# Two mixture-of-experts loops on one core: the first block written apart, and the pause moved from behind block 7 to behind block 12

## What is computed

```python
# first block: 16 experts, 2 of one group of 4 for each token, no biases
for e in range(N_EXPERTS):
    h = jax.nn.silu(t @ w_gate[e]) * (t @ w_up[e])
    y = y + gate_dense[:, e:e + 1] * (h @ w_down[e])

# second block: 32 experts, 4 for each token, with biases on both products
gu = xb @ w_gu[e] + b_gu[e]
gate, up = gu[:, :1024], gu[:, 1024:]
gate = jnp.minimum(gate, 7.0)
up = jnp.clip(up, -7.0, 7.0)
ys = ((up + 1.0) * gate * jax.nn.sigmoid(1.702 * gate)) @ w_down[e] + b_down[e]
```

## Time and profile before

| | us |
|---|---|
| median of three executions | 2166.97 |
| the profiled execution | 2168.93 |
| span of its trace | 2167.1 |
| TensorE matmul busy | 2088.0 (96%) |
| TensorE weight loads busy | 903.1 (42%) |
| VectorE busy | 517.2 (24%) |
| ScalarE busy | 318.1 (15%) |

### The profile page before, as it was taken

How to read it: one execution, slowest core, us unless ns; L and a number is a source line. 1 busy time by engine, 2 the same in 40 slices (tenths; PEclk the granted TensorE clock), 3 DMA queues, 4 the chain that set the end, 5 groups by cost and what they waited for, 6 DMA issues and landing times.

```text
span 2167.1 us, 22836 instructions
## 1 busy us (share of the span) xinstructions
PE 2088.0 (96%) x8939; PEld 903.1 (42%) x8942; DVE 517.2 (24%) x1098; ACT 318.1 (15%) x487; POOL 44.0 (2%) x67
## 2 busy tenths in 40 slices
PE   8999999999999999999999999999999999999997
PEld 6754333343324465645565433333333333333332
DVE  0675211011113410001052422222222122212212
ACT  1531111010002032211042111111110011111000
POOL 2010000000001000000000000000000000000000
PEclk9999999999999999999999999999999999999999
DMA  9984999999998422334334499999999999999997
GB/s 372 353 328 160 368 429 429 427 406 429 428 429 322 141 81 90 106 102 155 124 153 165 161 411 429 429 429 429 428 429 428 429 429 429 429 428 429 428 429 300
DMA packets 83290, 720.54 MB, mean 332 GB/s; under 512 B 6411, under 2 KB 11776, under 8 KB 42640
## 3 DMA queue, kind: packets, MB, share of 16 engines
q1 hardware_dynamic: 80864, 713.76, 79.7%
q0 software_dynamic: 2384, 6.21, 1.0%
HBM read 718.87 MB, written 1.08 MB: 332 GB/s over the span
## 4 chain that ended last, share of the span: by engine, by line
PE 62%; DMA 33%; DVE 3%; ACT 1%; issue 1%; POOL 0%; SPq 0%; DVEq 0%; ACTq 0%
DMA ring<-in_exp_w_gu 26%; PE bank L832 14%; PE bank L842 10%; PE bank L440 10%; DMA ring<-in_w_up 7%; PE bank L470 4%; PE bank L532 3%; PE bank L1078 3%; PE bank L457 3%; PE bank L1089 3%; PE bank L849 2%; PE bank L812 2%; PE bank L824 1%; PE bank L1214 1%; PE bank L793 1%
## 5 line engine op out<-in xcount | busy, mean ns | idle before, releaser
L832 PE MATMUL bank<-ring,pool 128*64 128x512 f32 x2560 | 566.0, 595 | 13.3 <-DMA ring<-in_w_up 10.3
L842 PE MATMUL bank<-ring,pool 128*64 128x512 f32 x2048 | 451.6, 595 | 23.1 <-DMA ring<-in_exp_w_gu 23.1
L832 PEld LDWEIGHTS bank<-ring,pool 128*64 128x64 f32 x2560 | 177.0, 137 | 356.2 <-issue 333.1
L842 PEld LDWEIGHTS bank<-ring,pool 128*64 128x64 f32 x2048 | 141.7, 137 | 309.9 <-issue 253.6
L440 PE MATMUL bank<-ring,pool 128*128 128x512 f32 (+2 forms) x512 | 213.3, 576 | 1.3 <-issue 1.3
L440 PEld LDWEIGHTS bank<-ring,pool 128*128 128x128 f32 x512 | 96.9, 190 | 112.9 <-issue 105.9
L1614 ACT ACTIVATE pool<-pool 128x512 f32<-128x512 f32 x32 | 20.1, 629 | 740.3 <-DVE pool L2284 740.3
L2284 DVE TENSOR_SCALAR pool<-bank 128x512 f32<-128x512 f32 x32 | 22.1, 691 | 417.0 <-PE bank L842 417.0
L1457 ACT ACTIVATE pool<-bank 128x512 f32<-128x512 f32 (+1 forms) x104 | 60.4, 580 | 325.9 <-PE bank L1141 63.9
L849 PE MATMUL bank<-pool,junk 64*128 64x512 f32 x400 | 99.4, 615 | 2.6 <-ACT pool L1457 1.1
L812 PE MATMUL bank<-pool 128*64 128x512 f32 x384 | 93.0, 605 | 0.1
(11 more groups left out here) (394 smaller groups left out, 1511.9 us busy)
## 6 DMA issues: line engine op xcount, KB each, us to landing
ring<-in_exp_w_gu SPq DMA_DIRECT2D x128, 2048.0 KB, 23.8
ring<-in_exp_w_down SPq DMA_DIRECT2D x64, 2048.0 KB, 20.0
ring<-in_w_gate SPq DMA_DIRECT2D x32, 2048.0 KB, 18.8
ring<-in_w_up SPq DMA_DIRECT2D x32, 2048.0 KB, 21.2
ring<-in_w_down SPq DMA_DIRECT2D x32, 2048.0 KB, 17.1
ring<-in_w_in SPq DMA_DIRECT2D x21, 2048.0 KB, 7.8
ring<-in_ada_w SPq DMA_DIRECT2D x12, 2048.0 KB, 16.8
ring<-in_w_out SPq DMA_DIRECT2D x4, 2048.0 KB, 10.5
```

Source lines behind the costliest of these rows:

```text
L832: i = mm(dst[half[f], :], chunks[kk], weights[j][:, k, f * 512:(f + 1) * 512], start=(kk == 0), stop=(kk == KC - 1))
L842: i = mm(dst[half[f], :], chunks[2 * j + k], weights[j][:, k, at:at + 512], start=False, stop=(j == 3 and k == 1))
```

## The change

`SPLIT` goes from 7 to 12. Body 0 of both loops is written out apart as `first_block`, in another order, and the loops start at 1:

- In both stages the gather of block 1 comes first, ahead of the waits for `y_slot` and `put`.
- In m1 there is no scatter; an empty instruction increments the semaphore that it would have.
- In m2 `biases` moves from between `turn_hidden` and `turn_gathered` to behind the down product.

```diff
-        SPLIT = 7
+        SPLIT = 12
...
+                def first_block():
+
+                    pe.wait_ge(S(f"{m}_pick"), 2)
+                    gather()
+                    pe.wait_ge(S(f"{m}_y_slot"), 1)
+                    pe.wait_ge(S(f"{m}_put"), 1)
+                    if biased:
+                        scatter()
+                    else:
+                        pe.nop().then_inc(S("m1_scattered"), 1)
+                    pe.wait_ge(S(f"{m}_hid"), 2)
+                    turn_hidden()
+                    pe.wait_ge(S(f"{m}_rows"), 2)
+                    turn_gathered()
+                    pe.wait_ge(S(f"{m}_hidT"), 1)
+                    for j in (4, 5):
+                        pe.wait_ge(full[j], 16)
+                        product(DN, hid_chunks, j)
+                    if biased:
+                        pe.wait_ge(S("m2_expert"), 2)
+                        biases()
+                    pe.wait_ge(S(f"{m}_pick_g"), 1)
+                    pe.wait_ge(S(f"{m}_xgT"), 2)
+                    turn_put()
+                    for j in range(4):
+                        pe.wait_ge(full[j], 32)
+                        up(j)
+
...
+                first_block()
                 if m == "m1":
-                    blocks(0, SPLIT)
+                    blocks(1, SPLIT)
...
                 else:
-                    blocks(0, n - 1)
+                    blocks(1, n - 1)
```

## The result

The changed kernel takes 2170.73 us, the kernel before 2168.28 us (medians of 20 executions each); 2.45 us apart; the ratio, as it was estimated with its interval, is 1.0015, 95% interval 1.0009 to 1.0021. That is 2.0 to 4.5 us slower (3.25 in the middle), a loss clear of noise but hardly beyond the 0.2% that I had called the edge of "no change". The forecast was 3.6 us more, 2170.6 us. That the time itself was met within 0.2 us is partly luck: the forecast stood on 2166.97 us, the median of three executions, and twenty give 1.3 us more.

What follows compares the result with a forecast made beforehand. The prediction took the stream of weight loads to bind some bodies of m1 and most of m2, TensorE the rest. +6.0 - 1.5 - 0.9 = +3.6 us on 2166.97 gave 2170.6 us, range 2168.0 to 2173.2.

Steps and rivals of the forecast that it cites:

- The pause (+6.0): m1: moved behind block 12, only three bodies follow to use up the stream's lead; 6.0 us more.
- Rival C: m1: the ring pays for the pause wherever it stands, leaving only the gains, -2.4 us, 2164.6 us; chance 0.08.
- the whole hole of 2.98 us: m1, behind the pause after block 7: the stream's loss there, taken as all that the pause costs before the change.
- The first block of m1 (-1.5): m1's body 0: removing the scatter closes the stream's hole at 244 to 250; 1.50 us gained, bounds 1.0 and 1.91.
- One premise: m1's body 0: from a load's issue to its first byte take about 1.5 us.
- The first block of m2 (-0.9): m2's body 0: fifth unit asked for 1.57 us earlier, less a new 0.7 us hole; 0.9 us gained.
- only 1.1 to 1.2 us are in hand: m2, second body's fifth unit: the margin before the stream runs dry, so the earlier start opens a 0.7 us hole.
- rival B: Second body's fifth unit: holes move instead of closing, loads starting earlier drain earlier; +4.8 or +6.3 us; chance 0.23.
- Rival D: Loops of m1 and m2: shifted code forces instruction fetches at jumps back, +11 to +61 us on top; chance 0.03.

Runs made afterwards that it cites:

- e2: Kernel before with SPLIT = 12; m2's body 0 apart with scatter and biases behind the down product; 1.004 times before's time, m1 451.28 us, m2 916.64.
- e1: Changed kernel with the pause back behind block 7 and m2's body 0 back in its loop; 1.0001 times before's time, m1 444.70 us, m2 913.81.
- e9: Changed kernel with the pause behind block 10 and half the products of m2's block 0 unit 3 left out; m1 445.12 us, m2 912.84.
- e3: Changed kernel with m1's body 0 scatter kept, pause behind block 10, m2's biases behind the down product in every body; 298.54 us to the pause, m2 914.61.
- e5: Changed kernel with pause behind block 8, gather ahead of scatter in all bodies, m2's biases last in all; 0.9986 times before's time, 2166.09 us.
- e6: Changed kernel with pause behind block 5 and half the products of m2's block 1 units 1 and 2 left out; m1 444.55 us, m2 914.83.

## Why the prediction was right, and where it was wrong

**The pause (+6.0): right in kind, up to a microsecond too large.** Behind it the changed kernel took 95.74 us where 15.09 + 3 x 26.90 = 95.8 stood in the sum, and the five bodies ahead of it were bound by the stream at 29.37 us, as 568.30 - 538.93 = 29.37 in the chain. The table of m1 shows the mechanism whole. From block 5 to block 9 the place doesn't matter, 444.35 to 444.72 us. From block 10 on it costs 0.5, 3.5 and 5.3 us over the mean of those four (444.58); by the prediction's way of adding up, 15.1 us and the bodies at 26.90 and 29.37 us, the three would cost 1.1, 3.5 and 6.0. The kernels that differ in m1 by the pause's place alone say 4.95 (e2 against before) and 5.16 us (changed against e1) for block 12. The rest of the 6.0 lies ahead of block 7's place, where executions of the same code differ by about 1 us (209.70 and 208.70 in before and e2). Block 2 is too early: the stream had not yet got a lead, and the hole was 9.0 us. Rival C, the ring absorbing the pause wherever it stands, is refuted by blocks 2, 11 and 12. One step of the prediction doesn't come out: it has the pause behind block 7 cost the whole hole of 2.98 us, but 236.63 us are only 1.7 more than eight bodies at the stream's 29.37; no run shows where the other 1.3 went.

**The first block of m1 (-1.5): right, its size within the noise.** To block 7's place the three kernels with the scatter took 208.70 to 210.43, mean 209.61; the seven others with a pause behind block 5 or later and the scatter gone took 207.27 to 208.40, mean 207.83. The difference is 1.8 us, and the kernels of one group differ by up to 1.7 and 1.1 us among themselves, so it can't be told from 1.91, all that the scatter took of TensorE, nor from 1.50. Pairs with the pause at one place say 1.6 (e1 against before), 1.4 (changed against e2) and 2.9 us (e9 against e3). In the two profiles that I compared first it is 2.4, which is partly chance. One premise was rough: by the trace's time stamps the first packet of block 1's first load starts 0.97 us behind its request, not 1.5; the 1.5 us also hold the slow start. e3 shows that it is the removal: with the scatter kept, the gather's place gave nothing. What I had not seen is that the loss in GB/s is a sum over 16 engines. Unit 3 of block 5 of m1 had landed on its last engine 142.5 to 144.4 us behind the first request with the scatter, 141.2 to 142.3 without, by the same time stamps as above.

**The first block of m2 (-0.9): wrong.** It gave +0.24 in the profile, and in no kernel with the same requests was it a gain. The step that failed is "only 1.1 to 1.2 us are in hand": that the hole at the first place shrinks by the 1.57 us of the earlier request, that the second body's fifth unit gives 0.7 us back, and that there is no third place. The row of the kernel before at 1284 shows that nothing was in hand at the second place: the stream dips to 396 GB/s there already. In the changed kernel it dips to 374, and to 396 at a third place (1265), where the kernel before moves 437. The reports say what became of the gain. At unit 4 of block 1 the mean of the 16 engines was 1.2 us earlier than in the kernel before (28.6 and 29.8 us); from there to unit 3 of block 31 it needed 877.4 us instead of 876.4, and 0.2 us were left. That is rival B's mechanism: a load that starts earlier drains earlier, and the holes move.

Beneath it lies a second wrong reading, that a hole in the summed rate is a hole in what TensorE waits for. I worked out how long the stream would last from bytes over rate, as though the 16 engines were one. They aren't: when the last unit's first engine had reported, the last still took 0.7 to 4.2 us, and TensorE waits for the last. e3, e5 and e6, which ask for the second body's fifth unit 1.2 to 3.4 us earlier than the changed kernel, show it apart from the moving holes: their second dip is gone, and their mean engine kept its lead to the end of the stage (905.0 to 905.2 us against 906.2 in the kernel before), but the last engine came at 907.2 to 908.4, and m2 was no shorter. In all kernels with the request at 20.5 to 20.8 us the first engine got unit 4 at 27.7 to 28.1 instead of 29.4; the last engine got it at 29.9 to 30.8, the kernels with the late request at 30.1 and 31.0. Only when the request came at 19.06 was the last engine ahead of all these, at 28.5 and 28.9, and it kept that lead to the end of the stage (905.1 and 905.4 instead of about 907.4, or of 906.4 in e1). In m1 the request is at 19.2, which fits that the same edit gave its full worth there.

Rival B was right about the outcome (m2 gives nothing) and about the mechanism, but wrong that the second body's fifth unit decides alone: with that request earlier in e3, e5 and e6, m2 didn't follow. What remains open is why the engines' spread grows when a queue runs nearly dry, and how large it becomes in one execution; before's code alone gave 0.7 in one and 1.5 us in another, and its m2 differed by as much. Of e2's 2.1 us of loss 1.5 can be seen in the dip at 1266, where the next block's first units were asked for 1.7 us late.

**The sum.** +6.0 - 1.5 - 0.9 = +3.6 was forecast, +6.0 - 2.4 + 0.2 = +3.8 stands in the profile (its parts split at block 7's place), and +3.25 (2.0 to 4.5) in the times. By the pairs of kernels above it is rather +5.1 - 1.5 + 0.2. Either way two errors of about a microsecond had opposite signs: m2 gave 1.1 us less than forecast, and m1 lost 1.0 us less. That the sum came so near is luck; that it came out as a loss of a few microseconds is due to the pause, the only large term.

**Instruction fetch.** Rival D did not happen: the run has 29 packets instead of 28, and one of them (at 1285) falls into m2's loop behind 1262, 878 us long, against some 30 jumps back. The Trainium skill (Runtime: NRT & Kernel Launch, Instruction fetch mechanics) has the fetch forced where the target of a taken jump is out of the window; one packet against 30 jumps agrees with a loop that stays inside.

**The wait for 16.** The traces show 16 reports for every load of the two stages, 0.3 to 4.3 us from the first to the last. The Trainium skill (DMA: Bandwidth & Descriptors, Why a DMA increments its semaphore by 16 and not by 1) says that the engines finish independently and only the full 16 mean that all data has landed. The wait is for 16; the rate in the profile is a mean over 16.

## What to carry to other kernels

Work that is foreign to a loop bound by loads costs nothing more only as long as the loop's remaining bodies use up the lead that the stream gains in it. Take its length, less the time that the stream stands idle in it, divide by the body's slack, and put it more than that many bodies ahead of the end: here (15.09 - 2.98)/2.47 = 4.9 bodies, and five cost 0.5 us, six none. It mustn't come well before the stream binds either; here that is from the fifth body on. From block 5 to block 9 of 15 the place made no difference; block 12 cost 5.3 us and block 2 cost 6.5, and blocks 3 and 4 weren't tried.

A request that comes earlier was worth something here only when it came before the stream ran thin at all (19.1 us and not 20.5 in m2); short of that the holes moved, or the rate summed over the engines rose and the last one's landing stayed where it was. Look for every dip in the stretch ahead, not only the deepest. And where an effect is below the spread of whole executions, marks inside the trace, between two points that the edit brackets, settle much that twenty timings leave open; but they have a spread of their own, 0.7 us for m2 and about 1 us for m1's first half, and smaller effects need more than one trace.

## What the hardware showed that I had not expected

- The 16 DMA engines don't keep step. From block 3 of m2 on their spread stayed, within 0.2 us in every kernel, for the rest of a stage of 900 us: the first and the last report of unit 3 were 2.3 us apart in block 20 and 2.3 us apart in block 31 of the changed kernel, 4.2 and 4.2 us in e5.
- With the first engines 1.5 us earlier at the end (904.2 instead of 905.7, e3, e5 and e6 against before), m2 was no shorter in any of the three.
- m1's length repeated within 0.4 us (444.35 to 444.72 in four kernels that differ only in the pause's place, or in the order of a body), while the part ahead of it varied by 4.9 us from execution to execution, more than the whole change moved.
